# Second products of a layer's MLP and of two feed-forward blocks as seven half-size products instead of eight

## The reference, cut to what matters

```python
x = x + gt2[:, None, :] * (jnp.square(jax.nn.relu(h @ mlp_w1[i])) @ mlp_w2[i])    # 1024 -> 4096 -> 1024
...
def swiglu(h, w_gate, w_up, w_down):                                              # 1024 -> 2816 -> 1024
    return (jax.nn.silu(h @ w_gate) * (h @ w_up)) @ w_down
...
x = x + 0.5 * swiglu(rmsnorm(x, ffn1_norm[l]), ...)     # and once more, ffn2, at the end
```

## Time and profile before

| | us |
|---|---|
| median of 3 runs | 2538.02 (2536.36 to 2540.02) |
| profiled execution | 2542.36 |
| its span, first to last instruction | 2540.6 |
| TensorE busy | 2490.3 |
| VectorE busy | 1329.9 |
| ScalarE busy | 908.6 |
| mean granted TensorE clock | 0.988 |

### The profile page before, as it was taken

One profiled execution on the slowest core, in us unless ns is written; L12 is line 12 of the kernel. 1 busy time (PEld: TensorE's weight loads), 2 busy tenths in 40 slices (PEclk: granted clock), 3 DMA queues, 4 the chain that ended last, 5 costly groups with the idle time before them and its releaser, 6 DMA issues.

```text
span 2540.6 us, 39183 instructions
## 1 busy us (share of the span) xinstructions
PE 2490.3 (98%) x16966; PEld 2050.9 (81%) x16966; DVE 1329.9 (52%) x1967; ACT 908.6 (36%) x1364; POOL 201.8 (8%) x176
## 2 busy tenths in 40 slices
PE   9999999999999999999999999999999999999998
PEld 7888888876787887888888888888668987888887
DVE  7865746647845446543444544432345745444433
ACT  4224323337633233431433322322256444322221
POOL 1000000000220000000000111000221000111100
PEclk9999999999999999999999999999999999999999
DMA  8563665622210003232222332333112422322232
GB/s 341 192 197 117 200 197 185 189 86 81 85 39 4 5 29 126 82 108 99 93 100 75 108 100 95 91 97 124 64 48 76 141 79 65 114 92 99 87 100 71
DMA packets 79725, 271.86 MB, mean 107 GB/s; under 512 B 8912, under 2 KB 11216, under 8 KB 79040
## 3 DMA queue, kind: packets, MB, share of 16 engines
q1 hardware_dynamic: 67696, 224.79, 26.9%
q0 software_dynamic: 11856, 44.55, 5.5%
HBM read 265.11 MB, written 4.19 MB: 106 GB/s over the span
## 4 chain that ended last, share of the span: by engine, by line
PE 92%; DVE 5%; ACT 2%; issue 1%; DMA 0%; SPq 0%; DVEq 0%; ACTq 0%
PE ps L624 26%; PE ps L630 22%; PE ps L628 22%; PE ps L640 3%; PE ps L643 3%; PE ps L655 1%; DVE WLs L1780 1%; PE ps L796 1%; PE ps L809 1%; DVE ada L1796 1%; PE ps L597 1%; PE ps L822 1%; PE ps L693 1%; PE ps L1119 1%; PE ps L1133 1%
## 5 line engine op out<-in xcount | busy, mean ns | idle before, releaser
L1780 DVE TENSOR_TENSOR WLs<-raw,WHs 128x1024 fp32r<-128x1024 f32 (+2 forms) x406 | 461.4, 1137 | 419.4 <-ACT WHs L1218 418.7
L624 PE MATMUL ps<-HH,WHs 128*128 128x512 f32 x1728 | 646.6, 400 | 3.7 <-DVE Pq L2332 2.1
L1218 ACT ACTIVATE WHs<-raw 128x1024 fp32r<-128x1024 f32 (+2 forms) x424 | 416.7, 984 | 550.7 <-PE ps L630 444.7
L630 PE MATMUL ps<-HH,WLs 128*128 128x512 f32 x1406 | 548.3, 390 | 1.2 <-DVE WLs L1780 1.2
L628 PE MATMUL ps<-HL,WHs 128*128 128x512 f32 x1406 | 547.7, 390 | 0.0
L624 PEld LDWEIGHTS ps<-HH,WHs 128*128 128x128 f32 x1728 | 324.9, 189 | 76.0 <-issue 11.2
L630 PEld LDWEIGHTS ps<-HH,WLs 128*128 128x128 f32 x1406 | 263.9, 188 | 57.2 <-DVE WLs L1780 1.6
L628 PEld LDWEIGHTS ps<-HL,WHs 128*128 128x128 f32 x1406 | 264.4, 188 | 53.7 <-issue 2.2
L624 PE MATMUL ps<-HM,WHs 128*128 128x512 f32 x576 | 224.1, 389 | 0.0
L628 PE MATMUL ps<-HM,WHs 128*128 128x512 f32 x576 | 224.1, 389 | 0.0
L630 PE MATMUL ps<-HM,WLs 128*128 128x512 f32 x576 | 224.1, 389 | 0.0
(11 more groups left out here) (419 smaller groups left out, 3449.0 us busy)
## 6 DMA issues: line engine op xcount, KB each, us to landing
ada<-in_adaw POOLq DMA_DIRECT2D x80, 512.0 KB, 4.5
raw<-in_f1gu_m SPq DMA_DIRECT2D x38, 512.0 KB, 3.3
raw<-in_f2gu_m SPq DMA_DIRECT2D x38, 512.0 KB, 3.2
raw<-in_mw_0b SPq DMA_DIRECT2D x32, 512.0 KB, 3.5
raw<-in_mw_1b SPq DMA_DIRECT2D x32, 512.0 KB, 3.5
raw<-in_w_in_m SPq DMA_DIRECT2D x18, 512.0 KB, 3.3
ada<-in_adaw SPq DMA_DIRECT2D x16, 512.0 KB, 15.7
raw<-in_cw_in_m SPq DMA_DIRECT2D x16, 512.0 KB, 3.4
```

Of the source, the lines that this page charges most:

```text
L624: pe.matmul(o[m], WHs[:, s, w], hi, start=k == 0, stop=False)
L630: t = pe.matmul(o[m], WLs[:, s, w], hi, start=False, stop=k == DEPTH_K[name] - 1)
L1218: act.activation(WHs[:, SLOT[v], 0:n], raw_[:, v % NRAW, 0:n], ACT.Copy).then_inc(*S.up("w_hi", ("hi", v)))
L1780: dve.tensor_tensor(WLs[:, s, 0:n], raw_[:, v % NRAW, 0:n], WHs[:, s, 0:n].bitcast(F32), SUB).then_inc(*S.up("w_lo", ("lo", v)))
```

## The change

Second products are cut into quads: two output blocks, two halves of the depth, two halves of the tokens. A product of 2 x 2 by 2 x 2 sub-blocks takes eight sub-products; a quad makes seven (Strassen's scheme, in Winograd's form), each of 128 output features, half of the depth and 256 tokens, out of sums of weight quarters and sums of activation quarters. Kind "s" in `PROJ` marks them: the second products of layer 1's MLP (now three parts, of 12, 10 and 10 hidden blocks), and those of the feed-forwards (two parts each, of 12 and 10), but for `f2d_b`, which stays as it was, now with depth 10.

- TensorE: `fast` does seven products per quad in three PSUM banks. Three products go on top of a bank that has been drawn once, and wait for that draw.
- Weights: four quarters are loaded per quad. Of the seven pieces four are sums of quarters, made by VectorE in `sum_quarters`, just ahead of the low part of the piece in front.
- Activations: per pair of hidden blocks VectorE makes four half-width combinations (T1 at the even block, T3, T2, T4 at the odd one). High and low parts are then 256, 512, 512 and 512 columns per pair (`HT`), instead of 512 and 512. In `hidden_fast` the square is VectorE's, and each block's high and low parts lag by one block.
- Results: each product is drawn (`draw`) with a sign into its half of one X block; PSUM goes on accumulating in between. The closing of an X block (square sum, HL, second sum) comes after draws 5 and 6.
- The ring `pr` has three pairs; `GH` holds a weight sum now.

```diff
-        ("mw1_1a", "e", 16, 8), ("mw2_1a", "m", 8, 16), ("mw1_1b", "m", 16, 8), ("mw2_1b", "m", 8, 16),
-        ("f1gu", "f", 44, 8), ("f1d", "m", 8, 22),
+        ("mw1_1a", "e", 12, 8), ("mw2_1a", "s", 8, 12), ("mw1_1b", "m", 10, 8), ("mw2_1b", "s", 8, 10),
+        ("mw1_1c", "m", 10, 8), ("mw2_1c", "s", 8, 10),
+        ("f1gu_a", "f", 24, 8), ("f1d_a", "s", 8, 12), ("f1gu_b", "m", 20, 8), ("f1d_b", "s", 8, 10),
         ("w_in", "f", 24, 8), ("w_out", "g", 8, 8), ("wkv", "m", 16, 8), ("wq", "m", 8, 8), ("wo", "g", 8, 8),
-        ("f2gu", "f", 44, 8), ("f2d", "m", 8, 22)]
+        ("f2gu_a", "f", 24, 8), ("f2d_a", "s", 8, 12), ("f2gu_b", "m", 20, 8), ("f2d_b", "m", 8, 10)]
...
+BANK = [1, 2, 1, 3, 1, 2, 1]
+BEFORE = {2: 0, 4: 2, 5: 1, 6: 4}
+LAST_IN = {3: 3, 5: 2, 6: 1}
+
+DRAWS = [(0, 0, 1), (1, 1, -1), (1, 0, -1), (0, 0, 1), (1, 1, -1), (1, 0, -1), (0, 1, 1)]
+REDRAWN = {3: 0, 4: 1, 5: 2}
+
+INPUT = [0, 3, 1, 5, 2, 4, 6]
+INPUT_GROUP = [0, 2, 1, 3, 1, 2, 3]
+GROUP = [slice(0, 256), slice(256, 768), slice(768, 1280), slice(1280, 1792)]
+SUMMED = (1, 2, 4, 6)
...
+            def fast(name):
+                src = name.replace("mw2", "mw1")
+                for a in range(BLOCKS[name] // 2):
+                    o = {}
+                    for i in range(7):
+                        u, b, g = FIRST[name] + 7 * a + i, BANK[i], INPUT_GROUP[i]
+                        if b not in o:
+                            o[b] = bank(name, a, b, hold=True)[:, 0:256]
+                        else:
+                            on.wait_ge(*S.at("drawn", name, a, BEFORE[i]))
+                        s, n = SLOT[u], WANT[u][4]
+                        x = slice(256 * INPUT[i], 256 * INPUT[i] + 256)
+                        on.wait_ge(*S.at("hi", u))
+                        for k in range(n):
+                            w = slice(128 * k, 128 * k + 128)
+                            on.wait_ge(*S.at("ch", src, k, g))
+                            pe.matmul(o[b], WHs[:, s, w], HT[:, 0, k, x], start=k == 0 and i not in BEFORE, stop=False,
+                                      skip_group_check=i in BEFORE)
+                            on.wait_ge(*S.at("cl", src, k, g))
+                            pe.matmul(o[b], WHs[:, s, w], HT[:, 1, k, x], start=False, stop=False, skip_group_check=i in BEFORE)
+                            on.wait_ge(*S.at("lo", u))
+                            t = pe.matmul(o[b], WLs[:, s, w], HT[:, 0, k, x], start=False, stop=k == n - 1, skip_group_check=i in BEFORE)
+                        t.then_inc(*S.up("mm_dense", ("full", name, a, i), ("used", u)))
+                        if i in LAST_IN:
+                            B.release((name, a, b))
...
-            dense("mw1_1a", h, lambda k: ("HL", "m1", k))
-            dense("mw2_1a", hm, lambda k: ("mlo", "mw1_1a", k))
-            dense("mw1_1b", h, lambda k: ("HL", "m1", k))
-            dense("mw2_1b", hm, lambda k: ("mlo", "mw1_1b", k))
+            for part in "ab":
+                dense("mw1_1" + part, h, lambda k: ("HL", "m1", k))
+                fast("mw2_1" + part)
+            dense("mw1_1c", h, lambda k: ("HL", "m1", k))
+            if KIND["mw2_1c"] == "s":
+                fast("mw2_1c")
+            else:
+                dense("mw2_1c", hm, lambda k: ("mlo", "mw1_1c", k))
...
+            def high(src, k, g, x):
+                act.activation(HT[:, 0, k, GROUP[g]], x, ACT.Copy).then_inc(*S.up("a_in", ("ch", src, k, g)))
+
+            def hidden_fast(name):
+                def finish(m):
+                    k, x = m // 2, tmp_[:, m % 4]
+                    if m % 2 == 0:
+                        on.wait_ge(*S.at("t2", name, m))
+                        high(name, k, 0, x[:, early])
+                    else:
+                        on.wait_ge(*S.at("T4", name, k))
+                        high(name, k, 2, T2[:, 1])
+                        high(name, k, 1, T2[:, 0])
+                        high(name, k, 3, x)
...
+                    if v + 1 < len(WANT) and WANT[v + 1][1] == "s" and WANT[v + 1][3] in SUMMED:
+                        sum_quarters(v + 1)
...
+            def sum_quarters(v):
+                _, _, a, i, _ = WANT[v]
+                a11, a21, a22, a12 = (quarter(v, q) for q in range(4))
+                v0 = v - i
+                if i == 1:
+                    if a:
+                        on.wait_ge(*S.at("lo", v0 - 1))
+                    on.wait_ge(*S.at("raw", v0, 0))
+                    on.wait_ge(*S.at("raw", v0, 1))
+                    dve.tensor_tensor(piece(v), a11, a21, ADD).then_inc(*S.up("w_sum", ("sum", v)))
+                if i == 2:
+                    if a:
+                        on.wait_ge(*S.at("lo", v0 - 5))
+                    on.wait_ge(*S.at("sum", v0 + 1))
+                    on.wait_ge(*S.at("raw", v0, 2))
+                    dve.tensor_tensor(piece(v), piece(v0 + 1), a22, ADD).then_inc(*S.up("w_sum", ("sum", v)))
+                if i == 4:
+                    dve.tensor_tensor(piece(v), a21, a22, ADD).then_inc(*S.up("w_sum", ("sum", v)))
+                if i == 6:
+                    on.wait_ge(*S.at("lo", v0 + 1))
+                    on.wait_ge(*S.at("sum", v0 + 2))
+                    on.wait_ge(*S.at("raw", v0, 3))
+                    dve.tensor_tensor(piece(v), piece(v0 + 2), a12, ADD).then_inc(*S.up("w_sum", ("sum", v)))
...
+            def draw(name, a, i):
+
+                of, to, _ = RESIDUAL[name]
+                e, hf, sign = DRAWS[i]
+                m, b = 2 * a + e, BANK[i]
+                x = X[:, m, TOKENS[hf]]
+                on.wait_ge(*S.at("full", name, a, i))
+                on.wait_ge(*S.at("X", of, m))
+                if i in REDRAWN:
+                    on.wait_ge(*S.at("drawn", name, a, REDRAWN[i]))
+                if isinstance(GATE[name], tuple):
+                    on.wait_ge(*S.at("mod", 6 * GATE[name][0] + GATE[name][1]))
+                    on.wait_ge(*S.at("ngate"))
+                events = [("drawn", name, a, i)]
+                events += [("free", name, a, b)] if i in LAST_IN else []
+                events += [("X", to, m)] if i >= 5 else []
+                dve.scalar_tensor_tensor(out=x, in0=taken(name, a, b)[:, 0:256], scalar=gate(name, m) if sign > 0 else minus_gate(name, m),
+                                         in1=x, op0=MUL, op1=ADD).then_inc(*S.up("v_evac", *events))
...
+                    if isinstance(m, tuple):
+                        draw(name, *m)
+                        for n, b in closed(m):
+                            close(name, n, b)
+                        return
...
+            def first_combination(src, k, even, t1):
+
+                dve.tensor_tensor(t1, even[:, early], even[:, late], SUB).then_inc(*S.up("v_in", ("T1", src, k)))
+
+            def combinations(src, k, even, odd, t1, t2, t3, t4):
+                dve.tensor_tensor(t3, odd[:, late], even[:, late], SUB).then_inc(*S.up("v_in", ("T3", src, k)))
+                on.wait_ge(*S.at("T1", src, k))
+                dve.scalar_tensor_tensor(out=t2, in0=t1, scalar=-1.0, in1=odd[:, late], op0=MUL, op1=SUB).then_inc(*S.up("v_in", ("T2", src, k)))
+                on.wait_ge(*S.at("T2", src, k))
+                dve.scalar_tensor_tensor(out=t4, in0=t2, scalar=-1.0, in1=odd[:, early], op0=MUL, op1=SUB).then_inc(*S.up("v_in", ("T4", src, k)))
+
+            def low(src, k, g, x):
+                on.wait_ge(*S.at("ch", src, k, g))
+                dve.tensor_tensor(HT[:, 1, k, GROUP[g]], x, HT[:, 0, k, GROUP[g]].bitcast(F32), SUB).then_inc(*S.up("v_in", ("cl", src, k, g)))
...
+            def hidden_fast(name):
+                def finish(m):
+                    k, x = m // 2, tmp_[:, m % 4]
+                    if m % 2 == 0:
+                        low(name, k, 0, x[:, early])
+                    else:
+                        low(name, k, 2, T2[:, 1])
+                        low(name, k, 1, T2[:, 0])
+                        low(name, k, 3, x)
+
+                def evac(m):
+                    k, x = m // 2, tmp_[:, m % 4]
+                    on.wait_ge(*S.at("relu", name, m))
+                    dve.tensor_tensor(x, x, x, MUL).then_inc(*S.up("v_evac", ("t2", name, m)))
+                    if m:
+                        finish(m - 1)
+                    on.wait_ge(*S.at("t2", name, m))
+                    if m % 2 == 0:
+                        if k:
+                            on.wait_ge(*S.at("cl", name, k - 1, 1))
+                        first_combination(name, k, x, T2[:, 0, late])
+                    else:
+                        if k:
+                            on.wait_ge(*S.at("cl", name, k - 1, 2))
+                        combinations(name, k, tmp_[:, (m - 1) % 4], x, T2[:, 0, late], T2[:, 0, early], T2[:, 1, early], T2[:, 1, late])
+                    if m == BLOCKS[name] - 1:
+                        finish(m)
+                return evac
```

(37 more changed lines are left out.)

278 lines of the change are left out of this document (188 added, 90 removed), and 3 rows, old and new, of the table RESIDUAL.

## The result

The changed kernel takes **2575.24 us** (median, 2573.55 to 2581.09) beside 2537.94 for the one before on the same chip: 1.015 times as long, 95% interval 1.0137 to 1.0162. It is 37.3 us slower; forecast were 24.5. Its profiled span is 2574.6 us, 34.0 more than before. TensorE's idle time in it went from 50.3 to 89.7 us.

A forecast was written before the change was run, and what follows sets the result against it. TensorE's matmul stream was taken as the bound. Terms -27.2 + 5.3 + 22.1 + 13.4 + 8.5 + 0.4 + 2 gave +24.5 us on the median 2538.0: forecast 2562.5 us, range 2547 to 2576, chance 0.69.

The forecast's parts named there:

- Pitch and saving: TensorE in the changed second products: 256-column matmuls at 0.1199 us, seven products for eight, -27.2 us if nobody is late.
- The burst: Layer 1's first eight hidden blocks end together, so block 10's low part starts late: +5.3 us.
- The entries: Six stage starts: product 2 waits for VectorE's queue, 3.3 to 4.4 us each, +22.1 us.
- Closings in layer 1: Last part of layer 1: closing X blocks delays product 2 by 3.9 us per quad, +13.4 us.
- In the feed-forward: Closing X in the first feed-forward, without second sum: 2.4 us in three quads, then 1.2, +8.5 us.
- The end: Shorter last block in the second feed-forward leaves 1.8 instead of 2.9 us before the norm's sums: +0.4 us.
- The clock: Lower granted clock after TensorE's gaps: between 0 and 21 us, taken as +2 us.
- The rival with a fall at each stall: Clock falls at every TensorE gap, 1.4 us each, 21 us: 2581 us; chance 0.10.
- the queues absorb it: Rival: draws and combinations hide behind TensorE, stalls together stay under 27 us: faster, 2520 us; chance 0.14.
- The isolated matmul's pitch: Rival: matmuls take 0.2158 and 0.1092 us, so 12 us less, 2550 us; chance 0.03.
- Half of the stalls: Rival: entries and closings of X cost half as much, 2540.5 us, no change that can be told; chance 0.04.

The follow-up runs named there:

- the filled wait: Changed kernel with 12 or 16 unread matmuls into a spare bank at TensorE's waits for a quad's first draw: 2568.04 us, 1.0103 of the kernel before.
- the best version: Changed kernel with last parts of layer 1 and first feed-forward in full blocks, six blocks side by side, draws first, end's draw earlier: 2534.28 us, 0.9988 of kernel before.

## Why the prediction was right, and where it was not

It was right in its sign, and the time lies in its range, but 12.8 us above the forecast and only 0.8 us inside the upper end of 2576; the repeated run's 2576.52 is outside. That the range held is in part luck. Step by step:

**Pitch and saving.** The 256-column matmuls follow one another at 0.12 us (12 of them drawn as 1.58 us in the filled wait), as in the earlier trace rows. The cut itself is free, as layer 1 in dense parts showed. -27.2 stands.

**The burst,** 5.3: 2.71 + 1.96, with 0.16 to 0.26 for each, is 5.0 to 5.2. Right, and at the block named.

**The entries,** 22.1, or 3.3 for each of depth 10: in the one at 1222 product 2 starts 6.77 us behind product 0 (1222.38 - 1215.61) and could start after 30 x 0.12 = 3.60, so it is 3.17 late. Taken so, all six are 2.6, 3.2, 3.2, 3.8, 4.4 and 3.8 us late where 3.5, 3.3, 3.3, 3.8, 4.4 and 3.8 were forecast, 21 in all; only the first is off. Each of these waits, which I laid out as one, came in pieces but for the first. The order of VectorE's queue is shown as the cause: another order alone took the long piece from 1.83 to 0.53.

**Closings in layer 1,** 3.9 a quad: the quad from 1367.51 to 1383.93 took 16.42 us, forecast 16.5. **In the feed-forward,** 2.4: 1749.02 - 1734.04 = 14.98, forecast 15.0. The closest of all, from a layout of three queues with durations from the earlier trace rows.

**The end,** 0.4: the wait for the last square went from 1.60 to 3.04 us, 1.4 more. VectorE writes eight outputs of the first half (3.22 us in one go) ahead of the second half's draw. Before, this held the draw until 2531.07, 1.0 us after it was due; the shorter block is done earlier, and the draw at 2565.03 is 2.4 us late. This queue I had not laid out.

**The clock,** 2: this step failed. The clock loss rose by 15.4 us, 13.4 more than I took, and with the waits at 49.3 beside 49.7 this is the whole error (37.5 less 24.5 is 13.0). I had two waits as witnesses, one of 1.55 us after which the clock held and one of 3.60 after which it fell, and gave gaps of 1.9 to 2.7 to the shorter one. The rows did not carry this: I had myself put the bounds at 0 and 21. And the trace of the kernel before had a witness against it that the prediction does not use, a wait shorter than any of mine (with one of 0.64 us 1.6 us ahead of it) and half the clock behind it:

```profile
665.21 0.50 PE L630 MATMUL ps<-M0H,WLs 128*128 128x512 f32 x1 [0.90 <-DVE WLs L1780]
```
```profile
666.00:669.00 3.00, 3.00 (x9) 2.33 (x8) 1.28 (x3) 2.31 (x4) 0.78 (x2) 0.50 0.27 93
```

The rival with a fall at each stall, 21 us, was nearer in this term and in the time (2581 is 6 us away, 2562.5 is 13): seven places fell of the fifteen counted, five at 1.7 us and two at 3.4.

**The rivals.** That the queues absorb it is out: 49.3 us of waits. The isolated matmul's pitch is out. Half of the stalls is out.

**Left open:** why a wait brings the clock down in one place and not in another (below), and whether the first feed-forward's last part alone, whose closings in good order leave one wait of 0.44 us, would improve the best version; it was not run.

## What to carry to other kernels

When TensorE's work shrinks, ask what each product waits for in the *order* of the small queues, and lay them out instruction by instruction: it gave quads and five of six entries to some 0.1 us, where busy shares of 46% said there was room. If VectorE waits for ScalarE, move both or neither. Price each new pause of some 2 us on TensorE at its length plus about 1 us of lower clock (15.4 us over 15 such pauses here); either remove it by an order or fill it with matmuls into a spare bank.
